# Projections in chunks of 512, 512 and 64 tokens in place of 384, 384 and 320

## The chip, the core and the metric

The kernel runs on one core of a Trainium2 chip. The metric is the device time of one execution in microseconds. The engines are named as the profile names them: PE is TensorE (its weight loads are listed apart, as PEld), DVE is VectorE, ACT is ScalarE, POOL is GpSimd, SP is SyncE.

## What is computed

One layer of a hybrid decoder trunk, for 1024 prompt tokens and for 64 sample tokens (8 sequences of 8 tokens) that share the weights. Cut to what matters here:

```python
xn = rmsnorm(x, norm_pre)
z  = xn @ w_in                       # 1024 -> 13312, cut into the inputs of three branches
A  : dilated sliding-window attention, 3 groups x 4 heads of 128
B  : HGRN2 recurrence, 8 heads, state 128 x 128
C  : trailing means over 2, 4, 8, 16 positions, 4 groups of 128
merged = gate_a * (y_a @ w_br_a) + gate_b * (y_b @ w_br_b) + gate_c * (y_c @ w_br_c)
x_next = x + rmsnorm(merged @ w_out, norm_post)
```

The sample tokens go through the same projections as the prompt tokens; in attention they also read cached keys and values, and in the other two branches they start from a given state. All 1088 tokens (1024 + 64) stand side by side as columns of the normed, transposed input.

## The kernel before

**Projections.** Every matrix product with a weight matrix is cut into units of 128 output columns. A unit's weights are 8 blocks of 128x128 (4 blocks in 16 of the units, those of the merge of branches A and C). Weights and activations are each split into a high and a low part of the type float32r, and a unit adds up three products: high weight by high activation, high weight by low activation, low weight by high activation. So a unit of 8 blocks has 24 steps. The method `project` runs these steps for one chunk `c` of the tokens: `CHUNKS[c]` gives its first token and its width, the sum builds up in PSUM bank `c`, and each step is one matmul whose moving operand is the chunk's columns and whose stationary operand is a 128x128 block, loaded anew for each matmul. A unit therefore takes three passes over its 24 blocks, one for each chunk, and each pass loads all 24 blocks again.

**Conveyor.** SP loads a unit's weights, POOL splits them in two (`split`), PE multiplies (`project`), ACT copies each finished chunk out of its bank (`empty`, or `empty_ext` for the pooling inputs, where the prompt tokens and the sample tokens go to two places). Two slots hold weights, so the loads and splits of the next units run while PE works. A chunk's bank must be emptied (`bank_free`) before the next unit's same chunk starts; a consumer that needs a whole unit waits with `emptied`, by default for the last chunk.

**Order of PE's work.** It is written out by hand. The phases are norm, attention (4 heads), HGRN (8 heads), pooling, merge of B, merge of A and C, output. In attention and HGRN, chunks or half chunks (`half=0` and `half=1`, 12 steps each) of the next units are placed between the small matmuls of the head, so that PE has something to do while DVE prepares the next operands. In `head` of the HGRN phase one half chunk stands after each of the first four levels of products, in the order of the list `halves`: the second half of chunk 0, both halves of chunk 1, the first half of chunk 2.

**Norm phase.** For nine tiles of tokens (eight of 128, one of 64) DVE norms a tile, PE transposes it (L450), ACT and DVE split it into high and low (L401, L425). Unit 0's first two chunks are placed among the transposes, at the tiles where enough tokens are split:

```python
if t % 3 == 2 and t > 2:                 # t = 5 and t = 8
    pe.wait_ge(banks_free, 2 * (t - 2))
    cv.project(pe, 0, 0, t // 3 - 1, KO, x_hi, x_lo)
```

The lines of the rows below: L230 is the matmul in `project`; L243 and L244 are ACT's copies in `empty`, L310 to L313 those in `empty_ext`; L450 the transposes of the norm phase; L867 and L871 the level products of HGRN; L1380 and L1388 the transposes of cached keys and the scores of the sample tokens against them; L1960 the transposes of the output phase.

Of the kernel before, what the change touches and what calls it, by code (L numbers as in the profile page):

```python
# [29 lines left out]
ACT = mybir.ActivationFunctionType  # L30
# [4 lines left out]
KO = D // P  # L35
SEQ = 1024
NB, TB = 8, 8
NS = NB * TB
NT = SEQ + NS
TILES = SEQ // P  # L40
# [5 lines left out]
HIST = 15  # L46
# [6 lines left out]
COL_MG = COL_CG + GROUP  # L53


CHUNKS = ((0, 384), (384, 384), (768, NT - 768))
NCH = len(CHUNKS)
SLOTS = 2

# [46 lines left out]
def build(nc, A, OUT):  # L106
    ctx = ExitStack()
    with ctx:
        def sb(name, shape, dt=F32, scope=ctx):
            return scope.enter_context(nc.sbuf_tensor(name, list(shape), dt))  # L110

        def sem(name, scope):
            h = lot[0].enter_context(nc.semaphore(name))
            taken.append(h.num)
            return h
# [26 lines left out]
        psum = ctx.enter_context(nc.psum_tensor("psum", [P, 8, 512], F32))  # L142
# [12 lines left out]
        x_hi = sb("x_hi", (P, KO, NT), F32R)  # L155
        x_lo = sb("x_lo", (P, KO, NT), F32R)
# [11 lines left out]
        class Conveyor:  # L168
# [44 lines left out]
            def project(self, pe, u, s, c, nko, hi, lo, each=None, k0=0, half=None):  # L213
                t0, n = CHUNKS[c]
                steps = [(w_hi, x, k) for k in range(nko) for x in (hi, lo)] + [(w_lo, hi, k) for k in range(nko)]
                first, last = steps[0], steps[-1]
                if half is not None:
                    m = len(steps) // 2
                    steps = steps[m * half:m * (half + 1)]
                if half != 1:  # L220
                    if c == 0:
                        pe.wait_ge(self.hi_ready, u + (1 + self.u0))
                    pe.wait_ge(self.bank_free, u * NCH + (c + 1 + NCH * self.u0))
                for step in steps:
                    w, x, k = step
                    if w is w_hi and x is hi and each is not None:
                        pe.wait_ge(each, k0 + k + 1)
                    if w is w_lo and k == 0 and c == 0:
                        pe.wait_ge(self.split_done, u + (1 + SLOTS + self.u0))
                    mm = pe.matmul(psum[:, c, 0:n], w[:, s, k, :], x[:, k, t0:t0 + n],  # L230
                                   start=step is first, stop=step is last)
                if half != 0:
                    mm.then_inc(self.proj_done, 1)
# [5 lines left out]
            def empty(self, act, u, c, dst, func, raw=None):  # L239
                t0, n = CHUNKS[c]  # L240
                self.projected(act, u, c)
                if raw is not None:
                    act.activation(raw[:, t0:t0 + n], psum[:, c, 0:n], ACT.Copy)  # L243
                act.activation(dst[:, t0:t0 + n], psum[:, c, 0:n], func).then_inc(self.bank_free, 1)  # L244
# [54 lines left out]
        EXT = HIST + SEQ  # L299
        SEXT = HIST + TB  # L300

        def samples(x):
            return x[:, EXT:EXT + NB * SEXT].rearrange("p (b t) -> p b t", t=SEXT)

        def empty_ext(cv, act, u, c, x):

            t0, n = CHUNKS[c]
            cv.projected(act, u, c)
            if c < NCH - 1:
                act.activation(x[:, HIST + t0:HIST + t0 + n], psum[:, c, 0:n], ACT.Copy).then_inc(cv.bank_free, 1)  # L310
            else:
                act.activation(x[:, HIST + t0:EXT], psum[:, c, 0:SEQ - t0], ACT.Copy)
                act.activation(samples(x)[:, :, HIST:SEXT],  # L313
                               psum[:, c, SEQ - t0:n].rearrange("p (b t) -> p b t", t=TB),
                               ACT.Copy).then_inc(cv.bank_free, 1)


        def norm_phase(then):
# [3 lines left out]
            with scope:  # L322
# [18 lines left out]
                banks_free = sem("banks_free", scope)  # L341
# [7 lines left out]
                cv = Conveyor("n", scope, (3,), 0)  # L349

                def rows(t):
                    return P if t < TILES else NS

                with nc.Block() as block:
                    @block.sync
                    def _(sp):
                        for t in range(TILES):
                            sp.dma_start(xt[:, t, :], A["x_prompt"][0, t * P:(t + 1) * P, :]).then_inc(x_in[t], 16)
                            if t == 0:
                                sp.dma_start(g_pre[:, :], A["norm_pre"].broadcast_to([P, D])).then_inc(g_in, 16)  # L360
                                sp.dma_start(ident[:, :], A["c_ident"]).then_inc(ident_in, 16)
                            if t == 2:
                                cv.load(sp, 0, 0, then[0])
                        sp.dma_start(xt[0:NS, TILES, :], A["x_sample"].rearrange("b t d -> (b t) d"))\
                            .then_inc(x_in[TILES], 16)
                        cv.load(sp, 1, 1, then[1])
                        for dst, src in ((band[:, :], A["c_band"]), (pair[:, :], A["c_pair"]),
                                         (h_norm[:, :], A["hgrn_norm"].rearrange("a p -> p a")),
                                         (p_scale[:, :], A["pool_scale"][0].rearrange("(g p) -> p g", p=P))):
                            sp.dma_start(dst, src, allow_slow_non_contiguous=True).then_inc(const_in, 16)  # L370
                        sp.dma_start(lg[:, :], A["hgrn_lb_logits"][0].rearrange("(h p) -> p h", p=P),
                                     allow_slow_non_contiguous=True).then_inc(lb_in, 16)
                        sp.wait_ge(const_in, 16 * N_CONST)
# [64 lines left out]
                    @block.tensor  # L438
                    def _(pe):
                        pe.sem_inc(Conveyor.proj_done, SLOTS * NCH)  # L440
                        pe.wait_ge(ident_in, 16)
                        for t in range(TILES + 1):
                            n = rows(t)
                            pe.wait_ge(xn_ready, t + 1)
                            for m in (2 * t, 2 * t + 1):
                                if m >= RING:
                                    pe.wait_ge(banks_free, m - RING + 1)
                                for b in range(HALF):
                                    k = m % 2 * HALF + b
                                    mm = pe.transpose(psum[:, 3 + m % RING, b * n:b * n + n],  # L450
                                                      xt[0:n, t, k * P:(k + 1) * P], ident[0:n, 0:n])
                                mm.then_inc(xt_done, 1)

                            if t % 3 == 2 and t > 2:
                                pe.wait_ge(banks_free, 2 * (t - 2))
                                cv.project(pe, 0, 0, t // 3 - 1, KO, x_hi, x_lo)
                        pe.wait_ge(banks_free, 2 * (TILES + 1))
                        cv.project(pe, 0, 0, NCH - 1, KO, x_hi, x_lo)

# [225 lines left out]
        def hgrn_phase(ext, p_gate, p_graw, then):  # L685
# [10 lines left out]
            with scope:  # L696
# [70 lines left out]
                with nc.Block() as block:  # L767
# [21 lines left out]
                    def _(act):  # L789
# [49 lines left out]
                        for c in range(NCH):  # L839
                            empty_ext(cv, act, BH * UNITS, c, ext[0])  # L840
                        for c in range(NCH):
                            cv.empty(act, BH * UNITS + 1, c, p_gate, ACT.Sigmoid, raw=p_graw)
                        for c in range(NCH):
                            empty_ext(cv, act, BH * UNITS + 2, c, ext[1])
                        store_states(BH - 1)
                        root(BH - 1)
                        for c in range(NCH):
                            empty_ext(cv, act, BH * UNITS + 3, c, ext[2])
# [1260 lines left out]
```

## Time and profile before

| | us |
|---|---|
| median of two runs | 2102.85 |
| the two runs | 2101.33 and 2104.37 |
| span of the profiled execution, first to last instruction | 2099.2 |
| PE busy in the span | 2018.2 (96%) |
| weight loads busy | 1959.0 (93%) |
| DVE busy | 738.0 (35%) |
| POOL busy | 467.6 (22%) |
| ACT busy | 350.4 (17%) |

The profiled execution has no time of its own beside its span; the span is 3.65 us under the median of the runs, and that is taken as what lies around a span. Matmuls are pipelined and their recorded durations overlap: a row's "mean ns" is how long one matmul was in the engine, and how fast matmuls follow one another is read from the difference of two start times.

### The profile page before, as it was taken

The page shows a single profiled execution, that of the slowest core. Times are in us where ns is not written, and L with a number is a line of the kernel's source. Part 1 is how long each engine was busy: PE and PEld are TensorE (multiplying, and loading weights), DVE is VectorE, ACT ScalarE, POOL GpSimd, SP SyncE. Part 2 cuts the span into 40 slices and gives each one's busy share as a digit, 9 for nine tenths or more (in the row PEclk, how much of TensorE's full clock was granted, in tenths as well). Part 3 has the DMA queues.
Part 4 walks back from the last instruction along what each step waited for, and adds up shares of the span by engine and source line. Part 5 has one row for each costly group of instructions (what it writes and reads, how often), then busy time and mean ns, then how long its engine had stood idle before and what let it go on. Part 6 is the DMA issues. An engine that isn't in the chain of part 4 may idle for free. (4 is left out here: it accounts for less than half of the span.)

```text
span 2099.2 us, 33247 instructions
## 1 busy us (share of the span) xinstructions
PE 2018.2 (96%) x12872; PEld 1959.0 (93%) x12872; DVE 738.0 (35%) x1306; ACT 350.4 (17%) x795; POOL 467.6 (22%) x276
## 2 busy tenths in 40 slices
PE   6999999999999999999999999998899999999796
PEld 6999999999999999999999999998899999999796
DVE  5224124122412415445445545534500132222324
ACT  5121122011111100110110110111211121111221
POOL 2211121121121111111111111112233323333220
PEclk9999999999999999999999999999999999999898
DMA  4312312222231221111111111213521132212612
GB/s 150 107 49 59 102 48 60 71 74 67 51 103 37 61 77 35 58 41 51 52 47 45 56 58 29 62 33 104 173 72 61 62 126 72 82 57 82 217 38 85
DMA packets 243966, 152.86 MB, mean 73 GB/s; under 512 B 34861, under 2 KB 231853, under 8 KB 243884
## 3 DMA queue, kind: packets, MB, share of 16 engines
q1 hardware_dynamic: 206012, 117.85, 19.2%
q10 hardware_dynamic: 37872, 33.79, 4.9%
q8 instruction: 67, 1.10, 0.2%
q14 instruction: 15, 0.12, 0.0%
HBM read 117.19 MB, written 34.42 MB: 72 GB/s over the span
## 5 line engine op out<-in xcount | busy, mean ns | idle before, releaser
L230 PE MATMUL psum<-x_hi,w_hi 128*128 128x384 f32 (+1 forms) x2688 | 889.7, 336 | 23.9 <-DVE x_lo L2020 10.5
L230 PE MATMUL psum<-x_lo,w_hi 128*128 128x384 f32 (+1 forms) x2688 | 871.2, 329 | 0.0
L230 PEld LDWEIGHTS psum<-x_hi,w_hi 128*128 128x128 f32 x2688 | 510.7, 190 | 39.9 <-issue 24.4
L230 PEld LDWEIGHTS psum<-x_lo,w_hi 128*128 128x128 f32 x2688 | 510.8, 190 | 0.0
L230 PE MATMUL psum<-x_hi,w_lo 128*128 128x384 f32 (+1 forms) x2688 | 497.8, 326 | 0.0
L204 POOL CAST w_hi<-w_raw 128x1024 fp32r<-128x1024 f32 (+1 forms) x136 | 136.5, 1004 | 1578.2 <-PE psum L230 1289.2
L230 PEld LDWEIGHTS psum<-x_hi,w_lo 128*128 128x128 f32 x2688 | 451.1, 188 | 0.0
L206 POOL TENSOR_TENSOR w_lo<-w_raw,w_hi 128x1024 fp32r<-128x1024 f32 (+1 forms) x136 | 330.8, 2433 | 10.9
L244 ACT ACTIVATE a_feature<-psum 128x384 f32<-128x384 f32 (+1 forms) x108 | 50.6, 474 | 391.8 <-PE psum L230 391.6
L871 PEld LDWEIGHTS psum<-b_q_decayed,b_k_decayed 128*128 128x128 f32 (+1 forms) x816 | 95.9, 188 | 5.1 <-issue 2.3
L871 PE MATMUL psum<-b_q_decayed,b_k_decayed 128*128 128x64 f32 (+1 forms) x816 | 98.0, 271 | 0.1
L244 ACT ACTIVATE c_ext<-psum 128x384 f32<-128x384 f32 (+1 forms) x96 | 45.2, 474 | 243.2 <-PE psum L230 234.2
L656 DVE TENSOR_TENSOR c_ext<-c_ext,c_gate_raw 128x1088 f32<-128x1088 f32 x12 | 18.6, 1553 | 177.5 <-ACT c_ext L244 177.5
L656 DVE TENSOR_TENSOR c_ext<-c_ext,c_gate 128x1088 f32<-128x1088 f32 x12 | 18.5, 1540 | 177.1 <-ACT c_ext L244 177.1
L230 PE MATMUL psum<-mb_y_hi,w_hi 128*128 128x384 f32 (+1 forms) x192 | 62.2, 329 | 2.4 <-DVE mb_y_lo L680 2.4
L230 PE MATMUL psum<-mac_y_lo,w_hi 128*128 128x384 f32 (+1 forms) x192 | 62.4, 329 | 0.0
L230 PE MATMUL psum<-mb_y_lo,w_hi 128*128 128x384 f32 (+1 forms) x192 | 62.3, 329 | 0.0
L230 PE MATMUL psum<-mac_y_hi,w_hi 128*128 128x384 f32 (+1 forms) x192 | 62.3, 328 | 0.0
L1597 DVE COPY s_q<-a_feature 128x64 f32<-128x64 f32 x12 | 9.0, 748 | 147.2 <-ACT a_feature L244 147.2
L1604 DVE TENSOR_TENSOR a_prob<-psum,band 128x128 f32<-128x128 f32 (+1 forms) x64 | 21.5, 378 | 103.7 <-PE psum L1344 102.8
L1344 PE MATMUL psum<-a_feature 128*128 128x128 f32 (+1 forms) x192 | 52.9, 439 | 0.0
L1344 PEld LDWEIGHTS psum<-a_feature 128*128 128x128 f32 x192 | 44.1, 280 | 4.6
(214 smaller groups left out, 1950.5 us busy)
## 6 DMA issues: line engine op xcount, KB each, us to landing
w_raw<-in_w_in SPq DMA_DIRECT2D x104, 512.0 KB, 3.9
s_cached<-in_cache_kv_w SPq DMA_DIRECT2D x128, 64.0 KB, 2.5
s_cached<-in_cache_kv_w SPq DMA_DIRECT2D x64, 128.0 KB, 2.4
merged_rows<-c_ext ACTq DMA_DIRECT2D x15, 544.0 KB, 2.7
spare<-branch_outputs SPq DMA_DIRECT2D x10, 544.0 KB, 5.9
branch_outputs<-b_gate ACTq DMA_DIRECT2D x8, 544.0 KB, 3.2
c_ext<-merged_rows SPq DMA_DIRECT2D x8, 544.0 KB, 3.7
xt<-in_x_prompt SPq DMA_DIRECT2D x8, 512.0 KB, 8.6
```

Source lines behind the costliest of these rows:

```text
L204: pool.tensor_copy(w_hi[:, s, 0:nko, :], w_raw[:, s, 0:nko, :]).then_inc(self.hi_ready, 1)
L206: pool.tensor_tensor(w_lo[:, s, 0:nko, :], w_raw[:, s, 0:nko, :], w_hi[:, s, 0:nko, :].bitcast(F32), ALU.subtract)\
L230: mm = pe.matmul(psum[:, c, 0:n], w[:, s, k, :], x[:, k, t0:t0 + n], start=step is first, stop=step is last)
L244: act.activation(dst[:, t0:t0 + n], psum[:, c, 0:n], func).then_inc(self.bank_free, 1)
L656: ins = dve.tensor_tensor(pb[p][:, :], pb[p][:, :], gt[p][:, :], ALU.mult)
L871: mm = pe.matmul(bank[0:w, b * wq:(b + 1) * wq], kr[:, ts], second(q[:, ts], n), start=True, stop=True)
L1344: mm = pe.matmul(bank[:, a:a + w], tokens(DST[U_Q[g]], g, c), keys(DST[U_K[g]], g, c), start=True, stop=True)
L1597: ch.step(dve.tensor_copy(dst[:, g, :], src[:, SEQ:NT]))
L1604: ins = dve.tensor_tensor(prob[:, a:a + w], ps_, mask, ALU.add)
```

## The change

The two prompt chunks become 512 tokens wide, and the third chunk holds the 64 sample tokens alone. A unit still has three chunks, so the count of matmuls and of weight loads stays as it was. `empty_ext` loses one copy, since its last chunk no longer holds prompt tokens. In the norm phase chunk 0 is now placed after tile 6 (it needs tiles 0 to 3) and chunk 1 after all transposes (it needs tiles 4 to 7).

```diff
-CHUNKS = ((0, 384), (384, 384), (768, NT - 768))
+CHUNKS = ((0, 512), (512, 512), (SEQ, NS))
...
             else:
-                act.activation(x[:, HIST + t0:EXT], psum[:, c, 0:SEQ - t0], ACT.Copy)
                 act.activation(samples(x)[:, :, HIST:SEXT],
-                               psum[:, c, SEQ - t0:n].rearrange("p (b t) -> p b t", t=TB),
+                               psum[:, c, 0:n].rearrange("p (b t) -> p b t", t=TB),
                                ACT.Copy).then_inc(cv.bank_free, 1)
...
-                            if t % 3 == 2 and t > 2:
-                                pe.wait_ge(banks_free, 2 * (t - 2))
-                                cv.project(pe, 0, 0, t // 3 - 1, KO, x_hi, x_lo)
+                            if t == 6:
+                                pe.wait_ge(banks_free, TILES)
+                                cv.project(pe, 0, 0, 0, KO, x_hi, x_lo)
+                        pe.wait_ge(banks_free, 2 * TILES)
+                        cv.project(pe, 0, 0, 1, KO, x_hi, x_lo)
                         pe.wait_ge(banks_free, 2 * (TILES + 1))
                         cv.project(pe, 0, 0, NCH - 1, KO, x_hi, x_lo)
```

## Rows read from the trace of the kernel before

**Rows 1.** The page: engines' busy time, share of the span, instructions.

```profile
span 2099.2 us, 33247 instructions
PE 2018.2 (96%) x12872; PEld 1959.0 (93%) x12872; DVE 738.0 (35%) x1306; ACT 350.4 (17%) x795; POOL 467.6 (22%) x276
```

**Rows 2.** The chain that ended last, in order: start us, us, what.

```profile
2006.93 11.89 PE psum L230 x72
2018.82 0.98 PE psum L1960 x9
```

**Rows 3.** Groups of matmuls by line, L230: busy us, mean ns, idle before.

```profile
L230 PE MATMUL psum<-x_hi,w_hi 128*128 128x384 f32 (+1 forms) x2688 | 889.7, 336 | 23.9 <-DVE x_lo L2020 10.5 <-ACT c_gate L244 6.7 <-ACT a_feature L244 5.4
...
L230 PE MATMUL psum<-mac_y_lo,w_hi 128*128 128x384 f32 (+1 forms) x192 | 62.4, 329 | 0.0
```

**Rows 4.** Timeline of PE in unit 1: start us, us, what.

```profile
48.61 0.33 PE L230 MATMUL psum<-x_hi,w_hi 128*128 128x384 f32 x1
...
52.77 0.31 PE L230 MATMUL psum<-x_hi,w_hi 128*128 128x320 f32 x1
...
56.29 0.34 PE L230 MATMUL psum<-x_hi,w_hi 128*128 128x384 f32 x1
```

**Rows 5.** Groups of weight loads by line and shape: busy us, mean ns.

```profile
L230 PEld LDWEIGHTS psum<-x_hi,w_lo 128*128 128x128 f32 x2688 | 451.1, 188 | 0.0
L871 PEld LDWEIGHTS psum<-b_q_decayed,b_k_decayed 128*128 128x128 f32 x768 | 91.4, 191 | 3.4 <-issue 2.3 <-DVE b_k_decayed L1028 0.2
...
L867 PEld LDWEIGHTS psum<-b_q_decayed,b_k_decayed 128*64 128x64 f32 x128 | 8.1, 138 | 2.0 <-issue 2.0
...
L1960 PEld LDWEIGHTS psum<-ident,c_ext 128*128 128x128 f32 x64 | 7.4, 141 | 1.0 <-ACT c_ext L244 0.8
```

**Rows 6.** Timeline of PE in three stretches of small matmuls.

```profile
147.37 1.84 PE L1388 MATMUL psum<-s_q,s_k_feature 128*128 128x8 f32 x16
149.07 1.07 PE L1380 MATMUL psum<-ident,s_cached 128*128 128x128 f32 x8
...
953.49 2.12 PE L871 MATMUL psum<-b_q_decayed,b_k_decayed 128*128 128x64 f32 x18
955.54 0.44 PE L230 MATMUL psum<-x_hi,w_hi 128*128 128x384 f32 x1
...
979.75 1.15 PE L867 MATMUL psum<-b_q_decayed,b_k_decayed 128*64 128x64 f32 x16
980.82 0.44 PE L230 MATMUL psum<-x_hi,w_hi 128*128 128x384 f32 x1
```

**Rows 7.** Timeline of PE at the lower clock, 43 us.

```profile
43.81 0.52 PE L230 MATMUL psum<-x_hi,w_hi 128*128 128x384 f32 x1
44.13 0.52 PE L230 MATMUL psum<-x_lo,w_hi 128*128 128x384 f32 x1
```

**Rows 8.** Busy time by window: PE, PEld, DVE, ACT, POOL, granted clock, DMA.

```profile
43.40:45.70 2.30, 2.30 (x8) 2.30 (x8) 0.00 (x0) 0.26 (x1) 0.00 (x0) 0.50 1.06 303
147.40:149.00 1.60, 1.60 (x17) 1.60 (x16) 0.00 (x0) 0.49 (x1) 0.00 (x0) 1.00 0.00 0
```

**Rows 9.** Timeline of PE in the norm phase.

```profile
21.92 1.97 PE L450 MATMUL psum<-ident,xt 128*128 128x128 f32 x8 [0.62 <-DVE xt L417]
23.54 0.67 PE L230 MATMUL psum<-x_hi,w_hi 128*128 128x384 f32 x1
...
39.12 1.34 PE L230 MATMUL psum<-x_hi,w_lo 128*128 128x320 f32 x8
43.00 0.69 PE L230 MATMUL psum<-x_hi,w_hi 128*128 128x384 f32 x1 [2.55 <-ACT a_feature L244]
```

**Rows 10.** Timeline of DVE in the norm phase: tile 6 is normed.

```profile
23.16 3.12 DVE L417 SCALAR_TENSOR_TENSOR xt<-xt,rs,g_pre 128x1024 f32<-128x1024 f32 x1
```

**Rows 11.** Groups of ACT's copies by line and shape.

```profile
L244 ACT ACTIVATE a_feature<-psum 128x320 f32<-128x320 f32 x36 | 15.8, 439 | 115.2 <-PE psum L230 115.2
...
L313 ACT ACTIVATE c_ext<-psum 128x64 f32<-128x64 f32 x4 | 0.9, 223 | 0.0
```

## The prediction, made before the result was known

> **What bounds the kernel now.** The first view is the page's shares of engine time: PE works nearly all of the span, its weight loads nearly as long, and no other engine passes 35% [rows 1]. Shares of overlapping matmuls say little, so the second view is the chain that ended last, in order of time: in the output phase it runs on PE alone, unit after unit of 72 matmuls in 11.89 us with nine transposes between them [rows 2]. The third is the groups of matmuls by line: three groups of 2688 at L230 and six of 192 (three products in each of the two merge phases), so 9216 matmuls, which is 3072 steps of three chunks, or 128 units of 24 steps. The idle time ahead of the largest group is 23.9 us in all [rows 3]. 128 units of 11.9 us are some 1520 us, nearly three quarters of the span. One nanosecond on a step is therefore 3.07 us at the end, and the question is what a step costs when its three matmuls are 512, 512 and 64 columns wide. All three chunks together have 1088 columns before and after, and as many matmuls and weight loads.
>
> **What a matmul costs, by its width.** The reader must take distances between starts, not durations. One 384-wide chunk of 24 matmuls runs from 48.61 to 52.77, 173.3 ns a matmul; the 320-wide one from 52.77 to 56.29, 146.7 ns [rows 4]. A step is 2 x 173.3 + 146.7 = 493.3 ns. The difference of 64 columns is 26.6 ns, 0.416 ns a column, which is one column per cycle at 2.4 GHz. What is left of 173.3 after 384 x 0.416 = 159.7 is 13.6 ns, a fixed part for each matmul. By that line a 512-wide matmul costs 226.6 ns. The bounds: at the lower clock 384 columns follow one another in 320 ns [rows 7] at a granted clock of 0.50, the 1.2 GHz level [rows 8], which is the bare streaming time with no fixed part; so below stands 512 x 0.416 = 213 ns, and above it the time in proportion, 173.3 x 512 / 384 = 231 ns. I take 226.6, since two widths at the full clock lie on that line.
>
> **The 64-wide matmul is the disputed cost.** By the same line it would be 64 x 0.416 + 13.6 = 40 ns. But each matmul brings its own load of a 128x128 block, and no load of these projections has stood behind so short a stream. Three neighbours in the trace show what such a stream does. The sample scores stream 8 columns behind a 128x128 load, and 16 of them take 1.70 us, 106 ns each, though 8 columns are next to nothing. The level products with 64 columns and a 128x128 load take 2.05 us for 18, 114 ns each. With a load of 64 columns in place of 128, 16 take 1.07 us, 67 ns each [rows 6]. So behind short streams the pace is set by the load, and it goes with the load's columns. These neighbours are plain float32, the projections float32r; the bridge is the duration of the load: 188 ns in the projections against 191 for the level products, while a 64-column load takes 138 and the loads of the transposes 141 [rows 5]. A float32r load thus looks like the slow kind. I take 110 ns, the middle of 106 and 114. Below stands 40 (load wholly hidden), above 137 (load and stream one after the other, 110 + 27).
>
> The Trainium skill, "TensorE: Matmul & The Clock Gate", section "Back-to-back issue gap", gives a matmul's gap alone as N/2.4 + 2.5 ns, with a floor of about 25 ns for up to 64 columns; as an estimate from that, a step would be 2 x 216 + 29 = 461 ns. The row of 384 columns speaks against it, 173.3 where it gives 162.5, and so do the 8-column rows.
>
> **The sum for the steps.** 2 x 226.6 + 110 = 563.2 ns against 493.3, so 69.9 ns more a step, and times 3072 it is +214.7 us. In words: the two wide chunks take in 53.3 ns each what their 128 further columns need, and the narrow one gives back only 36.7 of the 106.6 that its 256 lost columns would be worth, because its load then comes into view. Nothing hides this: PE is the chain.
>
> **Smaller edits.** In the norm phase chunk 0 moves behind tile 6. DVE ends tile 6's norming at 23.16 + 3.12 = 26.28 [rows 10], while PE now starts chunk 0 at 23.54, right behind tile 5's transposes, which take 1.62 us at the lower clock. So PE would wait to 26.3, turn tile 6 to 27.9, run chunk 0 with some matmuls at the lower clock (5.4 + 1.2) to 34.5, turn tiles 7 and 8 (some 2.4) to 36.9, and end chunks 1 and 2 (5.4 + 2.6) near 45. Now unit 0 ends near 40.3 [rows 9]. That is +4.7, of which 1.7 is in the sum already: +3. The idle 2.55 us behind it is ACT's start in the next phase and stays. If DVE is not yet through with tile 7's low part, 1 us more.
>
> ACT's copy of the last chunk shrinks from 439 ns to 223 [rows 11]; where PE or DVE waits for a unit's last chunk, 0.2 us earlier at some ten places, -2. The longer copies of 512 lie under 5.4 us of PE work. One copy less in four pooling units, off the chain: 0.
>
> In HGRN the half chunks cover DVE's updates. The first half of chunk 2 was 12 x 146.7 = 1.76 us and becomes 12 x 110 = 1.32, and if DVE just fits now, PE waits 0.4 us in each of 8 heads, +3.5; the other half chunks grow by 0.64 us and cover waits elsewhere, 0 to -4. I take 0. POOL's splits and the weight loads get longer units to hide in: 0.
>
> Total: span 2099.2 + 214.7 + 3 - 2 = 2314.9, and with the 3.65 us that lie between the span and the median, 2318.6; I say 2319 us, +10%.
>
> **The rivals.**
> - *The load stays hidden even behind 64 columns* (not slower). Then each matmul pays its stream and 13.6 ns whatever its width, a step is 2 x 226.6 + 40.2 = 493.4, and the time is 2104. What decides is the 64-wide pace: up to 54 ns the change is within 2% (42 us over 3072 steps is 13.7 ns; about what a measurement of this kernel can tell from no change). For it: 13.6 ns is all that is seen of a load under 320 columns. Against it: 106 ns behind 8 columns. No change also follows if load and stream never overlap, since the sums are then the same in any cut; but 384 columns and a load of about 110 would then take 270 ns, not 173.3. Both together 5%. The Trainium skill states a rule by which load and stream would not overlap here ("TensorE: Matmul & The Clock Gate", section "Measured speedup vs the span model": a load runs beside a matmul only when their row groups differ); the trace disagrees, with 173.3 ns.
> - *The fixed part goes as well*: the wide streams cost 213 and the narrow one its bare 27, a step 453, which is 40 ns less, 1980 us. For it: at the lower clock no fixed part is seen [rows 7]. Against it: 384 and 320 columns show one at the full clock, and 8 columns take 106 ns: 3%. The gap rule of the Trainium skill, cited above, would come out near this.
> - *float32r loads are as quick as those of the transposes.* Then 64 columns go at the 67 ns of the half-size load: a step 520, +82, 2186 us. The durations, 188 against 141, speak against it: 6%.
> - *Load and stream add up behind 64 columns*: 137 ns, a step 590, +298, 2402 us: 4%.
> - *The clock falls in the narrow chunks*, in which PE streams 27 of 110 ns. At the 1.2 GHz level the chunk would take 24 x 220, 2.6 us more; in every unit that is +338 beside the forecast, 2657 us. The 16 sample scores, which stream less still, ran at a granted clock of 1.00 [rows 8], but for 1.7 us, not 2.6: 4%. In the attention heads, where a narrow chunk now stands between such scores, a fall or two would be 3 to 10 us, within the range.
>
> **How the numbers follow.** The forecast, load-bound at 100 to 120 ns, has the other 78%. Its range comes from the bounds: 512 columns at 213 to 231 ns are -83 to +27 us, the narrow matmul's 106 to 114 are 12 either way, the edges 5. That gives 2235 to 2360; I carry the top to 2400, toward the case in which load and stream add up. Left out are the quick load, the two cases without a loss and the falling clock, 18%. Slower by over 2%: 92%; within: 5%; faster: 3%.
>
> **What will show it.** In the chain of the output phase a unit of 72 matmuls should take 13.5 us, not 11.89. In the timeline, 24 matmuls of 512 columns should take 5.4 us and 24 of 64 columns 2.6; PE's recorded busy share should stay near 96%, since it still never rests. The granted clock should stay at 1.00 through the merge phases. The first term fails if 512 columns pay no fixed part, the second if the narrow chunk is done in under 1.6 us or takes over 3; the edges fail if PE's idle time grows by more than 10 us.

## The result, and the profile after

The changed kernel takes 2372.18 us (2367.44 to 2376.93, two runs) against 2102.85: 1.129 times the kernel before, 95% interval 1.125 to 1.133. It is slower by 269 us, where 216 were forecast (2319 us, range 2235 to 2400). The profiled execution's span is 2375.1 us, a little above the median of the runs.

The page after, first part, answers to [rows 1]:

```profile
span 2375.1 us, 33243 instructions
PE 2297.6 (97%) x12872; PEld 1984.4 (84%) x12872; DVE 741.7 (31%) x1306; ACT 350.4 (15%) x791; POOL 471.4 (20%) x276
```

PE has as many instructions as before, is as busy, and takes 279 us longer over them. DVE, ACT and POOL do what they did. The weight loads' busy time is almost unchanged, 1984 against 1959 us, but now there are stretches in which no load runs, under the long streams.

The chain that ended last, in the output phase, answers to [rows 2]:

```profile
2316.86 0.98 PE psum L1961 x9
2317.85 13.63 PE psum L230 x72
2331.47 0.98 PE psum L1961 x9
```

A unit of 72 matmuls takes 13.63 us where it took 11.89, and the nine transposes beside it still take 0.98. Times 128 units the 1.74 us are 223 us of the 269.

Where in a unit they lie shows in the timeline of PE in one unit of that phase, which answers to [rows 4]:

```profile
2273.80 0.47 PE L230 MATMUL psum<-x_hi,w_hi 128*128 128x512 f32 x1
...
2277.54 1.98 PE L230 MATMUL psum<-x_hi,w_lo 128*128 128x512 f32 x8
2279.35 0.19 PE L230 MATMUL psum<-x_hi,w_hi 128*128 128x64 f32 x1
2279.38 0.28 PE L230 MATMUL psum<-x_lo,w_hi 128*128 128x64 f32 x1
2279.49 0.28 PE L230 MATMUL psum<-x_hi,w_hi 128*128 128x64 f32 x1
2279.60 0.28 PE L230 MATMUL psum<-x_lo,w_hi 128*128 128x64 f32 x1
...
2281.95 0.48 PE L230 MATMUL psum<-x_hi,w_hi 128*128 128x512 f32 x1
```

Read the starts. Eight 512-wide matmuls from 2277.54 to 2279.35 are 226 ns each. Then the narrow chunk: the first two matmuls start 0.03 us apart; after that the starts are 0.11 us apart, and the chunk takes 2.60 us for 24, 108 ns each, though 64 columns stream in 27. The weight loads of the same stretch show why the first is the exception:

```profile
2279.13 0.19 PEld L230 LDWEIGHTS psum<-x_hi,w_hi 128*128 128x128 f32 x1
2279.36 0.19 PEld L230 LDWEIGHTS psum<-x_lo,w_hi 128*128 128x128 f32 x1
2279.46 0.19 PEld L230 LDWEIGHTS psum<-x_hi,w_hi 128*128 128x128 f32 x1
```

The first narrow matmul's load ran from 2279.13, under the wide stream before. The second's load starts only with the first narrow matmul, at 2279.36, and from there loads and matmuls go in step, 0.11 us apart. It is plain in the durations too: a matmul of 64 columns is listed with 0.28 us, longer than the first, which found its weights ready, with 0.19.

The other 46 us are not in the merge and output phases. Busy time from the first matmul of the merge to the end, before and after (columns as in [rows 8]):

```profile
1502.60:2099.20 596.60, 563.40 (x3386) 558.31 (x3384) 134.23 (x101) 105.25 (x206) 179.36 (x106) 0.97 0.27 90
1698.70:2375.10 676.40, 647.16 (x3387) 548.86 (x3386) 137.12 (x102) 104.72 (x206) 184.28 (x106) 0.97 0.24 80
```

That stretch is 80 us longer, which is 46 units x 1.74, at the same granted clock. The rest lies ahead of it, and the mean granted clock, before and after, tells of it:

```profile
core 0: 2099.2 us, clock 0.985
core 0: 2375.1 us, clock 0.955
```

With levels of 1.00 and 0.50 that is some 214 us at the lower level after and 63 us before. The windows of the first HGRN head show where it falls (columns as in [rows 8]); the last line is a stretch of the merge of B:

```profile
909.70:913.10 3.40, 3.40 (x30) 3.19 (x29) 1.32 (x5) 0.60 (x1) 0.00 (x0) 1.00 0.01 2
913.10:923.40 10.30, 9.70 (x38) 8.91 (x38) 5.01 (x10) 0.22 (x1) 3.25 (x2) 0.50 0.01 2
923.40:930.00 6.60, 6.60 (x45) 5.90 (x43) 2.02 (x4) 0.60 (x1) 0.15 (x1) 1.00 0.27 79
...
1700.00:1890.00 190.00, 190.00 (x992) 161.30 (x991) 15.76 (x8) 19.84 (x42) 54.83 (x28) 1.00 0.22 71
```

And the timeline of PE around that fall:

```profile
909.54 2.12 PE L872 MATMUL psum<-b_q_decayed,b_k_decayed 128*128 128x64 f32 x18
911.59 0.30 PE L230 MATMUL psum<-x_hi,w_hi 128*128 128x64 f32 x1
...
913.72 3.67 PE L872 MATMUL psum<-b_q_decayed,b_k_decayed 128*128 128x64 f32 x16 [0.60 <-DVE b_k_decayed L1029]
917.15 0.40 PE L230 MATMUL psum<-x_hi,w_hi 128*128 128x64 f32 x1
...
919.71 0.77 PE L230 MATMUL psum<-x_hi,w_hi 128*128 128x512 f32 x1
```

Level products of 64 columns, half a narrow chunk, level products again, the other half: four short-stream pieces in a row. At the end of the second of them the clock goes to the lower level. The next 16 products take 3.43 us to the following start, where 18 such took 2.05 us before [rows 6], the second half chunk takes 2.56 us, and the clock comes back during the wide matmuls. PE was idle for 0.60 us in that stretch, no more.

### The profile page after: what moved, and what is told of

It is laid out like the page before. It is cut to its first block and busy times, and to the rows that moved or that the text cites. A ratio compares the mean times of both kernels' runs of the same rounds, so it can differ in the third digit from the quotient of the medians.

```text
span 2375.1 us, 33243 instructions
## 1 busy us (share of the span) xinstructions
PE 2297.6 (97%) x12872; PEld 1984.4 (84%) x12872; DVE 741.7 (31%) x1306; ACT 350.4 (15%) x791; POOL 471.4 (20%) x276
## 5 line engine op out<-in xcount | busy, mean ns | idle before, releaser
L230 PE MATMUL psum<-x_hi,w_hi 128*128 128x512 f32 (+1 forms) x2688 | 945.1, 367 | 27.6 <-DVE x_lo L2021 8.7
L230 PE MATMUL psum<-x_lo,w_hi 128*128 128x512 f32 (+1 forms) x2688 | 930.2, 361 | 0.0
L230 PEld LDWEIGHTS psum<-x_hi,w_hi 128*128 128x128 f32 x2688 | 525.8, 196 | 116.4 <-issue 31.1
L230 PEld LDWEIGHTS psum<-x_lo,w_hi 128*128 128x128 f32 x2688 | 525.5, 195 | 71.9
L230 PE MATMUL psum<-x_hi,w_lo 128*128 128x512 f32 (+1 forms) x2688 | 571.6, 356 | 0.0
L230 PEld LDWEIGHTS psum<-x_hi,w_lo 128*128 128x128 f32 x2688 | 455.1, 194 | 71.4
L244 ACT ACTIVATE a_feature<-psum 128x512 f32<-128x512 f32 (+1 forms) x108 | 50.9, 473 | 457.0 <-PE psum L230 456.7
L244 ACT ACTIVATE c_ext<-psum 128x512 f32<-128x512 f32 (+1 forms) x96 | 45.3, 473 | 283.3 <-PE psum L230 277.6
L230 PE MATMUL psum<-mac_y_hi,w_hi 128*128 128x512 f32 (+1 forms) x192 | 65.8, 356 | 0.0
L230 PE MATMUL psum<-mac_y_lo,w_hi 128*128 128x512 f32 (+1 forms) x192 | 65.6, 355 | 0.0
L230 PE MATMUL psum<-mb_y_hi,w_hi 128*128 128x512 f32 (+1 forms) x192 | 65.3, 356 | 0.0
L230 PE MATMUL psum<-mb_y_lo,w_hi 128*128 128x512 f32 (+1 forms) x192 | 65.2, 355 | 0.0
```

## The experiments

The theory after the result: (1) a matmul costs the longer of its stream plus 13.6 ns and its weight load of some 110 ns, so a step with a 64-wide matmul pays for streaming that doesn't happen; (2) the rest is the clock, which falls where narrow chunks stand beside other short streams. The rivals: that it is the 512-wide chunks which are dear, or the very short matmul as such, or that load and stream add up; and, for the rest, that the clock falls because of PE's waits on DVE. All experiments but e6 start from the changed kernel.

**e1: no chunk narrow, one still 512 wide.**

```diff
-CHUNKS = ((0, 512), (512, 512), (SEQ, NS))
+CHUNKS = ((0, 512), (512, 320), (832, NT - 832))
```

(`empty_ext` gets its second copy back, here and in e2.)

> Chunks of 512, 320 and 256: one chunk stays 512 wide, and none is narrow enough to be paced by its weight load. Theory (the load of about 110 ns sets the pace only where the stream is shorter): a step costs 226.6 + 146.7 + 120.1 = 493.4 ns, as much as 384, 384, 320, so the time is 2105 us, within 10 of the kernel before, and the low-clock time falls back to near 63 us. Rival (it is the 512-wide chunks that are dear, by their bank-filling matmuls or their longer copies): half of the loss stays, about 2240 us.

Measured: 2122.02 us, 1.0083 (1.0062 to 1.0104) times the kernel before. The unit in the chain of the output phase:

```profile
2013.69 11.86 PE psum L230 x72
```

11.86 us against 11.89, so the step is as cheap as with 384, 384, 320, and 512 columns are not dear in themselves. The rival is out. The 19 us that remain are more than the 10 that the expectation allowed: in attention the hand-written order gives DVE too little cover at one place, as the group of v-row transposes of the sample tokens shows (before, 0.4 us of idle time stood ahead of it):

```profile
L1355 PE MATMUL psum<-ident,a_feature 128*64 128x128 f32 x24 | 6.8, 281 | 11.3 <-DVE s_prob_t L1709 10.3 <-DVE s_prob L1685 0.6
```

11.3 us of idle PE stand there, and behind the longest of them the granted clock drops (0.72 in the window of 12 us around it). Some 4 us more are the norm phase's new order (e6). In all PE's idle time in the span went from 81.0 to 92.1 us and its busy time from 2018.2 to 2025.2. Which chunk's cover was short was not followed up.

**e2: a third chunk of 128 columns, 64 of them prompt tokens.**

```diff
-CHUNKS = ((0, 512), (512, 512), (SEQ, NS))
+CHUNKS = ((0, 512), (512, 448), (960, NT - 960))
```

> Chunks of 512, 448 and 128. Theory: 128 columns stream for 53 ns and so still wait for their load, 110 ns as with 64 columns; a step is 226.6 + 200.0 + 110 = 536.6 ns, 43 more than before, +133 us, 2236 us, plus up to 40 us where the clock falls. Rival 1 (load and stream add up behind a short stream): 128 columns cost 110 + 53 = 163 ns, a step 590 ns, 2400 us. Rival 2 (what is dear is the very short matmul, not the load): 128 columns cost 66.8 ns, a step 493.4 ns, 2105 us.

Measured: 2263.93 us, ratio 1.0768 (1.0735 to 1.0801). The timeline of PE in a narrow chunk:

```profile
2060.27 0.28 PE L230 MATMUL psum<-x_lo,w_hi 128*128 128x128 f32 x1
2060.38 0.28 PE L230 MATMUL psum<-x_hi,w_hi 128*128 128x128 f32 x1
2060.50 0.27 PE L230 MATMUL psum<-x_lo,w_hi 128*128 128x128 f32 x1
```

The starts are again 0.11 us apart: 128 columns cost the same as 64, as they must if both wait for the same load. Load and stream do not add up (163 ns expected by that rival), and the stream alone (67 ns) does not set the pace. The unit in the chain takes 13.00 us, 1.11 more than before, times 128 142 us; measured are 161 with the falls of the clock (0.977).

**e4: the same narrow chunk with half of each weight load.** The kernel leaves out, for the sample tokens, half of the output rows of each unit in 22 of the 24 products.

```diff
-                    mm = pe.matmul(psum[:, c, 0:n], w[:, s, k, :], x[:, k, t0:t0 + n],
+                    m = P // 2 if n == NS and step is not first and step is not last else P
+                    mm = pe.matmul(psum[0:m, c, 0:n], w[:, s, k, 0:m], x[:, k, t0:t0 + n],
...
```

> As the changed kernel, but in the third chunk 22 of a unit's 24 matmuls load only the first 64 columns of their weight block and write only 64 of the 128 output rows, so the other half of the sample tokens' outputs holds two of 24 products. Theory (the narrow chunk is paced by its weight load, in proportion to the load's columns): such a matmul goes from 112 to 58 to 67 ns, a step costs 45 to 50 ns less, -140 to -150 us, 2225 us; the falls of the clock may stay. Rival (the 110 ns are a fixed cost of a short float32r matmul, whatever it loads): no change, 2370 us.

Measured: 2233.48 us, ratio 1.0619 (1.0576 to 1.0663), 139 us less than the changed kernel. The timeline of PE:

```profile
2149.82 0.22 PE L231 MATMUL psum<-x_lo,w_hi 128*64 128x64 f32 x1
2149.88 0.22 PE L231 MATMUL psum<-x_hi,w_hi 128*64 128x64 f32 x1
2149.94 0.22 PE L231 MATMUL psum<-x_lo,w_hi 128*64 128x64 f32 x1
```

0.06 us from start to start with 64 columns streamed as before: the narrow matmul's pace goes with the load's columns. A fixed cost of short matmuls is out. The edit halves the output rows together with the load, so this run alone does not tell these two apart; that the load is what is waited for rests on the rows above, in which loads and matmuls go in step.

**e3: the third chunk streams 256 columns, of which 64 are used.**

```diff
+OFF = (0, 0, 192)
...
-                    mm = pe.matmul(psum[:, c, 0:n], w[:, s, k, :], x[:, k, t0:t0 + n],
+                    mm = pe.matmul(psum[:, c, OFF[c] - more:OFF[c] + n], w[:, s, k, :], x[:, k, t0 - more:t0 + n],
...
```

(`more` is `OFF[c]`; the copies read from column `OFF[c]` on.)

> As the changed kernel, but the third chunk's matmuls stream 256 columns (the last 192 prompt tokens once more, and the 64 sample tokens), of which only the 64 sample columns are copied out: more columns, same count of matmuls and loads. Theory (part of the loss is the clock, which falls where narrow chunks stand beside other short streams, some 70 us): a step costs 8 to 10 ns more, +25 to +31 us, but the low-clock time goes from 216 us to near 70, about -70 us: 2330 us. Rival (the falls come from waits, not from the narrow streams): the falls stay and the time goes to 2400 us.

Measured: 2347.2 us, ratio 1.1157 (1.1126 to 1.1188): 25 us faster than the changed kernel while streaming 18% more columns. The chain's unit and the granted clock:

```profile
2229.30 13.82 PE psum L232 x72
```

```profile
core 0: 2346.4 us, clock 0.986
```

A unit costs 0.19 us more than the 13.63 of the changed kernel, 24 us in all; the mean clock is back at 0.986. So the lost clock was worth some 25 + 24 = 49 us. The forecast of 2330 took 70 us for it, which was too much. Part of what the clock gave back came in again as waiting: ahead of the key transposes PE waits 7.0 us for DVE in all, where it waited 5.5. That is 1.5 us of the 21; the rest was not followed up.

**e5, e7, e8: padding only where the clock fell.** In e5 the two half chunks that stand between level products in the HGRN heads (`pad=j == 0` in `meanwhile`); in e7 also five units of an attention head (`pad=j in (2, 4, 6, 7, 8)` in `chunk`); in e8 its last two units as well.

> As the changed kernel, but only in the HGRN heads, in the first unit of each head (whose two narrow half chunks stand between level products), the third chunk streams 256 columns. Theory: the fall of the clock in each of 8 heads (7 to 10 us at half clock, 72 us in all) goes, -36 us, and 192 padded matmuls cost 2 us: 2338 us. Rival (the falls come from DVE's longer wait at that place or from the level products themselves): no change, 2370 us.

Measured: 2341.88 us, ratio 1.1135 (1.1104 to 1.1167), 30 us less than the changed kernel. The timeline and the windows of the same head:

```profile
911.29 1.99 PE L874 MATMUL psum<-b_q_decayed,b_k_decayed 128*128 128x64 f32 x16 [0.45 <-DVE b_k_decayed L1031]
913.10 0.36 PE L232 MATMUL psum<-x_hi,w_hi 128*128 128x256 f32 x1
```

```profile
909.10:912.00 2.90, 2.45 (x20) 2.21 (x20) 2.50 (x6) 0.00 (x0) 0.00 (x0) 1.00 0.01 3
911.00:919.00 8.00, 7.71 (x56) 7.22 (x56) 4.62 (x10) 0.22 (x1) 3.41 (x2) 1.00 0.01 2
900.00:980.00 80.00, 79.55 (x497) 68.97 (x496) 38.52 (x72) 9.14 (x17) 13.66 (x8) 1.00 0.16 48
```

PE still waits 0.45 us for DVE at the place where it waited 0.60, and the clock stays at 1.00 (0.94 over the same 80 us of the changed kernel); the same 16 level products take 1.81 us to the next start, not 3.43. Nor is it the 0.15 us between the two waits: the next head of the changed kernel waits only 0.37, and its products are slow as well.

```profile
1001.53 3.37 PE L872 MATMUL psum<-b_q_decayed,b_k_decayed 128*128 128x64 f32 x16 [0.37 <-DVE b_k_decayed L1029]
```

So neither the wait nor the level products alone bring the clock down; it falls only where the half chunks between them are narrow.

> As e5_pad_hgrn, and in the attention heads the third chunk of the five units that stand ahead of or between small matmuls streams 256 columns as well. Theory (what the changed kernel loses beyond the price of the steps is the clock in the heads): the low-clock time goes from 141 us to near 70, -35 us, the padding costs 4 us, 2310 us, which is the kernel before plus the forecast price of the steps (2103 + 215 = 2318) within 10. Rival (the falls in attention come from waits on DVE): 2345 us.

Measured: 2338.79 us, ratio 1.1133 (1.1111 to 1.1155). The expectation of 2310 failed: the mean clock rose to 0.977, but falls in the attention heads remained, and some of what the others had cost came back as waiting for DVE (1.76 us ahead of the key transposes in each head, 0.95 to 1.27 in e5: 2.7 us in all). Why the rest of the forecast gain did not come is open. The windows of e7 on one of the falls that stayed:

```profile
204.00:207.90 3.90, 3.90 (x36) 3.69 (x35) 0.13 (x1) 1.42 (x4) 0.55 (x1) 1.00 0.00 0
207.90:211.30 3.40, 3.31 (x16) 2.77 (x16) 2.92 (x9) 0.00 (x0) 2.84 (x2) 0.50 0.30 87
```

In the first of them PE runs the narrow chunk of unit 9 (from 204.41) and the turning of the probabilities. That unit was among the two left narrow. The other fall of this head comes behind the narrow chunk of the last unit, where PE also waits 1.54 us for POOL's split. In e8, with that chunk at 256 columns, the wait stands there all the same, and the clock is 1.00 from 244 to 252 us. The two rows, e7 and e8:

```profile
247.58 0.49 PE L232 MATMUL psum<-x_hi,w_hi 128*128 128x512 f32 x1 [1.54 <-POOL w_hi L205]
248.23 0.49 PE L232 MATMUL psum<-x_hi,w_hi 128*128 128x512 f32 x1 [1.51 <-POOL w_hi L205]
```

> As e7_pad_heads, and in attention the last two units of a head (units 9 and 10), whose narrow chunks were left as they were and stand ahead of the turned probabilities and of the head's end, stream 256 columns in the third chunk as well. Theory (the two falls a head that e7 still had, each right behind one of these narrow chunks, come from them): low-clock time from 107 us to near 75, about -9 us, 2330 us; by the run with all chunks padded (2347 us) less the padding of the 92 units left narrow here (0.19 us each) it is 2330 too. Rival (those falls come from PE's wait at the head's end): 2340 us.

Measured: 2334.91 us (2328.48 to 2337.22), ratio 1.1103 (1.1081 to 1.1124).

```profile
core 0: 2326.7 us, clock 0.985
```

In the profiled execution the clock is where it was before the change; in the other four it is 0.981 to 0.983. The time lies between the two expectations; the intervals of e7 and e8 overlap, so what the last two units are worth in time stays open. Against the changed kernel all three paddings together give 37 us, and as they cost 36 units x 0.19 = 7 us, the clock had cost some 44. Of these e5 shows 32, its 30 and the 8 units' padding. From the first merge matmul to the end e8 and the changed kernel both take 676 us, so the gain lies wholly ahead of the merge.

**e6: the kernel before with the norm phase's new order alone.** Chunks stay 384, 384 and 320.

```diff
-                            if t % 3 == 2 and t > 2:
...
+                            if t == 6:
```

> The kernel before with its chunks of 384, 384 and 320, and only the new places of unit 0's chunks in the norm phase. Forecast of that edge: +3 us, 2106 us, with unit 0 ending near 43 us; rival (the waits at this place cost nothing, since the next phase starts with a wait anyway): 2103 us.

Measured: 2105.0 us, ratio 1.0017 (1.0006 to 1.0029), which is 1 to 6 us. PE's timeline at the start of unit 1, answering to [rows 9]:

```profile
44.16 0.46 PE L230 MATMUL psum<-x_hi,w_hi 128*128 128x384 f32 x1 [2.55 <-ACT a_feature L244]
```

Unit 1 starts 1.16 us later than the 43.00 of before, with the same wait of 2.55 ahead of it: the delay is passed on. It is within the 1 to 6 us; where the rest of the median's 4 us would lie the row does not show.

No version that beats the kernel before came out of this, and the experiments say why: 512, 320 and 256 cost as much a unit as 384, 384 and 320 (11.86 and 11.89 us), and the cuts with a chunk of 128 or 64 cost more (13.00 and 13.63).

## Why the prediction was right

**The 512-wide matmul.** Forecast 226.6 ns by a line through two widths; eight took 1.81 us, 226 ns. The line holds, fixed part included. In the output phase each wide chunk begins behind short streams; with its first matmuls, 0.23 to 0.31 apart, it takes 5.55 us, not 5.44, and that is why the unit came a little above the forecast 13.5, to 13.63.

**The 64-wide matmul.** Forecast 110 ns from plain float32 neighbours, by way of the load's duration; measured 108 a matmul over a chunk, 112 between two in the middle. The bridge (188 ns of a float32r load are like the 191 of the level products) carried; the rows of the loads, e2 and e4 together show that the load is the cause. The rivals of a hidden load (2104 us), a missing fixed part (1980), a quick float32r load (2186) and a load added to the stream (2402) are out. The Trainium skill, "TensorE: Matmul & The Clock Gate", section "LDWEIGHTS (loading the stationary operand)", gives the load as its columns divided by 1.2, as an estimate 107 ns for 128 and 53 for 64; the trace comes near, with 112 and 58 to 60. The Trainium skill's rule by which load and stream would not overlap stands on the page that the prediction names, but in its section "The mechanism"; the 173.3 ns of 384 columns speak against it, as the prediction says.

**The sum.** Forecast +214.7 us for the steps; 1.74 us x 128 = 223. This term was right within 4%.

**The edges.** Norm phase: forecast +3. In the changed kernel unit 1 starts 6.3 us after the 43.00 of [rows 9], of which 1.7 is unit 0's own price, so +4.6: chunk 0 took 7.7 us, not 6.6, and PE waited 0.9 us for DVE, the "1 us more" that the prediction named. (In e6, where the chunks are the old ones, it is 1.16 at this place and 4 in the median.) The row of unit 1's start in the timeline of PE:

```profile
49.32 0.62 PE L230 MATMUL psum<-x_hi,w_hi 128*128 128x512 f32 x1 [2.66 <-ACT a_feature L244]
```

HGRN: forecast 0 net; the wait ahead of level 4 appears, as expected, and the one ahead of the turned outputs goes. Of PE's waits the first line is from before and is gone after; the second is from after and was not there before:

```profile
PE psum L925 <- DVE b_o_rows L1108: 6.1, 7, 0.9
PE psum L872 <- DVE b_k_decayed L1029: 3.1, 8, 0.6
```

No run tried the 2 us for ACT's shorter copies alone.

**What was mis-sized: the clock.** The prediction had it as a rival that decides in every unit (2657 us, 4%), and within the forecast as "a fall or two" in the attention heads at 3 to 10 us. In the merge and output phases, where a narrow chunk stands between wide ones, the clock stayed at 1.00, so the rival as priced is out. But in the heads it did fall: 44 us by e8, 49 by e3, 32 of them in HGRN (e5). The step that failed is the listing of places: the prediction looked for narrow chunks between the 8-column scores of attention and overlooked that the third chunk's halves land between level products of 64 columns, though it had worked out the cover at that very place. With it, 2319 would have been about 2363.

**The range.** That the time fell inside it is partly luck. The bounds that the prediction worked out end at 2360, below the 2372 measured. The top was carried on to 2400 toward a load that adds to the stream, and e2 shows that this is not so; the clock took the time there. The low end is not the sum of its terms either: with 83, 12 and 5 us off, 2319 goes to 2219, not 2235.

## What to carry to other kernels

Where each matmul brings its own weight load, cost a cut by the longer of stream and load for each piece, not by the columns in all: the columns saved below the load's length are given away. Test the bound at another width: if the pace between starts doesn't move with the streamed columns and does with the loaded ones, the load sets it. And look at what stands next to a thin piece in the order of the work: in this kernel the clock fell behind short streams in a row, with PE busy for 3.40 of the 3.40 us before, and stayed at 1.00 where the same piece stood between wide ones.

## What the runs showed of the hardware

A kernel that streams more columns can be faster: 256 in place of 64 in every third matmul took 25 us off (e3), with the mean granted clock at 0.986 in place of 0.955.

In the first HGRN head the clock fell with PE busy for 3.40 of the 3.40 us before and with an idle time of 0.60 us at the fall. The Trainium skill, "TensorE: Matmul & The Clock Gate", section "HAM oscillation — how this bites in real kernels", looks for such falls behind idle gaps; here the row shows one where the only gap is that 0.60, and padding the streams, with a wait of 0.45 left, removed it (e5).

The fixed part of 13.6 ns a float32r matmul is seen at 320, 384 and 512 columns at the full clock and not at the lower one [rows 7]. What it is was not tried.
